# RWKV gate projection moved ahead of the recurrence, and the group norm written as factor times tile plus another tile

## Chip, cores and metric

One core of a Trainium2 chip runs the whole program. The metric is device microseconds of one execution, the median of several runs. Lower is better.

## What is computed

The reference is three transformer layers on 512 tokens of width 1024: an RWKV-7 layer with its MLP, a forgetting-attention layer with its MLP, and a hybrid sparse-attention layer with its MLP. The change touches the first layer's time mixing only. Cut to that:

```
g = sigmoid(x_g @ g1) @ g2                      # g1: 1024x160, g2: 160x1024
... y = recurrence over 512 tokens (16 heads of 64) ...
mean = mean(y over the head); var = mean(square(y - mean))
y = (y - mean) * rsqrt(var + GN_EPS)
y = y * lnx_w + lnx_b
bonus = sum(r * k * r_k over the head) * v
y = (y + bonus) * g
x = x + y @ w_o
```

## The kernel before

Activations lie transposed: a tile is 128 features by 512 tokens, and a full matrix is eight tiles (`DT`). Matrix products have float32 accuracy through three products of rounded parts: a weight block (128 x 1024) is split by GpSimd into `whi` and `wlo` (`split_hi`, `split_lo`), an activation into a high part (ScalarE, a rounding copy) and a low part (VectorE, a subtraction), and `three` issues high x high, high x low, low x high. A full output tile is 24 matmuls of 512 columns.

Weights come as one numbered stream of blocks in the order of `PHASES`: SyncE loads a block into one of four raw slots when GpSimd has split the block that was there, GpSimd splits it into one of two slots (`SPL`) when TensorE is done with the block before the last (`blk`), and TensorE waits for it on `split_ready`. Each engine's order is written out by hand, and semaphores tie the engines together.

The first layer runs in this order. A mixing stage prepares the inputs (`mix`, `mix_lo`) while TensorE makes k and r. Then come the eight value tiles (`for e in range(DT)` at line 693); between them `BETWEEN` puts the head sums of kk and of the bonus, and `kk_spread` hands the kk norm back to all rows. VectorE works meanwhile through a loop of eight (line 1872) that makes the operands of the recurrence and the bonus products (`bonus`; `bonus(i)` waits until the head sum of product i-2 is done, since two buffers `tmp` alternate). TensorE then transposes k, b and v to token order (`tokens`), and the recurrence follows in four steps of two chunks of 64 tokens (`for n in range(QT)`), each a long chain of small matmuls with ScalarE and VectorE between them.

After the recurrence comes the norm stage. TensorE makes head means with the block matrix `bones`, VectorE subtracts them (`gn_c`), ScalarE squares, TensorE sums by head (`head_sums`), ScalarE takes the root, VectorE the reciprocal and its two parts (`head_recip`). In a loop of eight TensorE then spreads the factor over the rows (`spread`, a matmul with 48 rows) and makes a tile of the gate projection (six matmuls: two weight blocks, the second with 32 live rows of 128). For each tile VectorE multiplies by the spread factor, ScalarE applies `lnx_w` and `lnx_b` (`gn_aff`), VectorE adds the bonus (`BON`) and multiplies by the gate out of PSUM (`y_gated`), ScalarE makes the high part and VectorE the low part. When all are through, `linear("rwkv_o", ...)` makes the eight output tiles one after another, and the residual, the next norm and the MLP follow. The gate's hidden values `sgF` get their parts `sgH` and `sgL` at the start of the norm stage. The two gate blocks are numbers 30 and 31 of the stream; GpSimd splits them in the last step of the recurrence, as its loop over the recurrence's masks stands ahead of them. The loads of x and of block 32 onward wait for the end of the recurrence (`rec_done`).

## Time and profile before

| | us |
|---|---|
| median of 3 runs | 2460.22 (2455.23 to 2460.65) |
| profiled execution, its own time | 2465.94 |
| its span in the trace | 2464.1 |
| TensorE busy (matmuls) | 2354.1, 96% of the span |
| VectorE busy | 1189.3, 48% |
| ScalarE busy | 573.7, 23% |
| GpSimd busy | 1289.0, 52% |

The profile is of one execution. A row of the page's groups gives line, engine, operation, tiles, count, busy time and the mean of one. The "chain that ended last" follows the last instruction back, at each step to what released it. A timeline row is start, length, engine, line and operation, and in brackets how long the engine had been idle and for whom. The granted clock is the share of TensorE's full speed (2.4 GHz); 0.50 is its lower level, 1.2 GHz. PE is TensorE, DVE VectorE, ACT ScalarE, POOL GpSimd.

### The profile page before, as it was taken

What the parts mean: (1) busy time and instruction counts of PE and PEld (TensorE: products, weight loads), DVE (VectorE), ACT (ScalarE), POOL (GpSimd) and SP (SyncE); (2) the same over time, 40 slices, a digit from 0 to 9 for tenths busy, and PEclk for the clock granted to TensorE, in tenths of its full rate; (3) what the DMA queues carried; (4) which work ended last, traced back from release to release, by engine and by line L of the source; (5) the groups of instructions that cost most, each with busy time, mean ns of one, the idle gap of its engine ahead of it and who ended that gap; (6) DMA issues with size and microseconds to landing.
All of it is one profiled execution on the core that took longest, in us unless ns stands there. A gap on an engine that the chain in (4) does not pass through costs nothing.

```text
span 2464.1 us, 41824 instructions
## 1 busy us (share of the span) xinstructions
PE 2354.1 (96%) x16908; PEld 1886.9 (77%) x16908; DVE 1189.3 (48%) x1483; ACT 573.7 (23%) x1168; POOL 1289.0 (52%) x839
## 2 busy tenths in 40 slices
PE   6988999899999999989999999999999999999999
PEld 4765888578888877766788888787877777888887
DVE  8858433475343352667543334518045656633333
ACT  4541333221010122144311111101015441201100
POOL 4652001056666655555566666566544545666665
PEclk9998999879999999999999999999998998999999
DMA  3220000122223222201222322223321111222222
GB/s 143 83 72 25 3 3 3 69 68 95 94 94 102 94 91 76 89 20 35 69 94 95 101 94 94 94 94 112 111 85 44 44 35 66 96 96 94 99 96 85
DMA packets 50448, 188.37 MB, mean 76 GB/s; under 512 B 5617, under 2 KB 5745, under 8 KB 49809
## 3 DMA queue, kind: packets, MB, share of 16 engines
q1 hardware_dynamic: 49824, 183.40, 22.2%
q10 hardware_dynamic: 496, 3.12, 0.4%
q8 instruction: 99, 1.62, 0.3%
q14 instruction: 29, 0.23, 0.0%
HBM read 184.33 MB, written 2.10 MB: 76 GB/s over the span
## 4 chain that ended last, share of the span: by engine, by line
PE 85%; DVE 10%; issue 2%; ACT 2%; POOL 0%; DMA 0%; ACTq 0%; DVEq 0%; SPq 0%; POOLq 0%
PE ps L593 23%; PE ps L595 22%; PE ps L594 22%; PE ps L1099 2%; PE ps L1084 2%; PE ps L768 2%; PE ps L605 2%; DVE HL L1948 1%; PE ps L1065 1%; DVE ssq L1745 1%; PE ps L778 1%; PE ps L1066 1%; PE ps L776 1%; PE ps L761 1%; PE ps L754 1%
## 5 line engine op out<-in xcount | busy, mean ns | idle before, releaser
L439 POOL TENSOR_TENSOR wlo<-raw,whi 128x1024 fp32r<-128x1024 f32 (+1 forms) x355 | 828.3, 2333 | 26.4
L432 POOL TENSOR_SCALAR whi<-raw 128x1024 fp32r<-128x1024 f32 x336 | 362.5, 1079 | 816.9 <-PE ps L595 792.3
L593 PE MATMUL ps<-HH,whi 128*128 128x512 f32 x1312 | 529.7, 404 | 8.4 <-DVE HL L1948 8.4
L595 PE MATMUL ps<-HH,wlo 128*128 128x512 f32 x1312 | 514.3, 392 | 0.0
L594 PE MATMUL ps<-HL,whi 128*128 128x512 f32 x1312 | 513.9, 392 | 0.0
L593 PEld LDWEIGHTS ps<-HH,whi 128*128 128x128 f32 x1312 | 248.1, 189 | 69.8 <-DVE HL L1948 14.1
L593 PE MATMUL ps<-hidH,whi 128*128 128x512 f32 x768 | 298.8, 389 | 0.0
L594 PE MATMUL ps<-hidL,whi 128*128 128x512 f32 x768 | 298.8, 389 | 0.0
L595 PE MATMUL ps<-hidH,wlo 128*128 128x512 f32 x768 | 298.8, 389 | 0.0
L595 PEld LDWEIGHTS ps<-HH,wlo 128*128 128x128 f32 x1312 | 248.2, 189 | 52.9
L594 PEld LDWEIGHTS ps<-HL,whi 128*128 128x128 f32 x1312 | 248.6, 189 | 52.3 <-issue 4.3
L1995 DVE TENSOR_TENSOR X<-X,ps 128x512 f32<-128x512 f32 x192 | 123.3, 683 | 306.7 <-PE ps L595 306.7
L1481 ACT ACTIVATE sqrT<-relT 128x512 f32<-128x512 f32 x96 | 60.8, 634 | 792.0 <-DVE relT L1984 792.0
L1987 DVE TENSOR_TENSOR hidL<-sqrT,hidH 128x512 fp32r<-128x512 f32 x96 | 183.9, 1935 | 88.8 <-ACT hidH L1485 88.8
L1984 DVE SCALAR_TENSOR_TENSOR relT<-ps,rstd 128x512 f32<-128x512 f32 x96 | 66.4, 692 | 234.1 <-PE ps L595 234.0
L594 PEld LDWEIGHTS ps<-hidL,whi 128*128 128x128 f32 x768 | 144.2, 188 | 30.0
L595 PEld LDWEIGHTS ps<-hidH,wlo 128*128 128x128 f32 x768 | 144.2, 188 | 29.9
L593 PEld LDWEIGHTS ps<-hidH,whi 128*128 128x128 f32 x768 | 144.2, 188 | 29.9
L465 POOL TENSOR_TENSOR mRB<-mRB,cst 128x512 f32<-128x512 f32 x8 | 10.1, 1279 | 176.2 <-ACT mRB L1435 176.2
L494 POOL TENSOR_SCALAR prs<-prs,cls,GT 128x32 f32<-128x32 f32 (+4 forms) x48 | 32.9, 686 | 78.0 <-DVE cls L2122 66.0
L593 PE MATMUL ps<-mixH,whi 128*128 128x512 f32 x128 | 52.8, 412 | 11.8 <-DVE mixL L1811 8.9
L1310 ACT ACTIVATE HH<-X,vec 128x512 fp32r<-128x512 f32 x40 | 28.8, 721 | 144.0 <-DVE X L1955 71.2
(438 smaller groups left out, 3598.6 us busy)
## 6 DMA issues: line engine op xcount, KB each, us to landing
raw<-stream SPq DMA_DIRECT2D x336, 512.0 KB, 3.3
X<-xT SPq DMA_DIRECT2D x2, 1024.0 KB, 6.6
X<-xT SPq DMA_DIRECT2D x1, 2048.0 KB, 7.7
CW<-cmpw ACTq DMA_DIRECT2D x1, 2048.0 KB, 10.2
out<-X SPq DMA_DIRECT2D x4, 512.0 KB, 2.6
cst<-consts SPq DMA_DIRECT2D x1, 511.5 KB, 9.3
c2f<-consts ACTq DMA_DIRECT2D x1, 466.0 KB, 3.2
c2s<-consts ACTq DMA_DIRECT2D x1, 466.0 KB, 5.4
```

What stands on the lines that cost most here:

```text
L432: pool.tensor_scalar(whi[:, s, :, :], raw[:, j, :].rearrange("p (k m) -> p k m", k=DT), 1.0, 0.0, ALU.mult, ALU.add)\
L439: return pool.tensor_tensor(wlo[:, s, a:z, :], raw[:, j, a * P:z * P].rearrange("p (k m) -> p k m", k=z - a), whi[:, s, a:z, :].bitcast(F3 ...
L593: pe.matmul(acc, whi[:, s, k, :], hi, start=start, stop=False)
L594: pe.matmul(acc, whi[:, s, k, :], lo, start=False, stop=False)
L595: return pe.matmul(acc, wlo[:, s, k, :], hi, start=False, stop=stop)
L605: pe.matmul(ps[0:112, bank, :], gather_heads(i), tmp[i % 2][:, :], start=i == 0, stop=i == n - 1).then_inc(S(f"{tag}_sum"), 1)
L768: mm = pe.matmul(square(hp, 1 - c, hp, p), mN[half(c), hp, p, :], mT[half(c), hp, p, :], start=True, stop=True)
L1084: mm = pe.transpose(ps[0:w, 4 + hp, j * P:(j + 1) * P], B["P"][:, 2 * (u % 2) + hp, j * P:j * P + w], ident)
L1481: act.activation(sqrT[:, j % 2, :], relT[:, j % 2, :], ACT.Square).then_inc(S("full"), 1)
L1984: dve.scalar_tensor_tensor(relT[:, j % 2, :], ps[:, j, :], 0.0, rstd[:, :], ALU.max, ALU.mult).then_inc(S("rel"), 1)
L1987: dve.tensor_tensor(hidL[buf][:, j - 1, :], sqrT[:, (j - 1) % 2, :], hidH[buf][:, j - 1, :].bitcast(F32), ALU.subtract).then_inc(S("hid"), 1)
L1995: ins = dve.tensor_tensor(X[:, e, :], X[:, e, :], ps[:, 4 + 2 * (j % 2) + o, :], ALU.add)
```

## The change

- The parts `sgH` and `sgL` of the gate's hidden values are made in the mixing stage, and in another place of SBUF.
- The 48 matmuls of the gate projection stand behind the eighth value tile, ahead of the transposes. They wait for both gate blocks to be split and alternate between two PSUM banks; ScalarE copies each tile to a new buffer `G`, which lies where the four raw weight slots are. GpSimd splits the two gate blocks ahead of its work for the recurrence.
- The bonus head sums go from behind value tiles 2 to 5 to behind tiles 3 to 6.
- In each step of the recurrence VectorE makes two tiles of (bonus + `lnx_b`) x gate in place of the bonus.
- In the norm stage, head means and head sums are interwoven (four PSUM banks for the means). VectorE makes the tiles `YA` = (y - mean) x `lnx_w` x gate, four of them ahead of the reciprocal. In the loop it multiplies one by the spread factor and adds the other tile. ScalarE's affine step is gone.
- The raw slots are loaded again as the `YA` tiles release `G`: blocks 32 and 33, then x, then 34 and 35, and from there on as before.
- Two output tiles are made side by side: in each of the eight steps of the loop TensorE does the same k for tile 0 and tile 1, with the spread for a later tile behind it. The other six tiles follow one by one.
- The semaphore for `gn_a` shares one with `sg_split`.

```diff
@@ -213,8 +213,10 @@
...
 
-    sgH = at("sgH", [P, 2, T], zone(7), F32R)
-    sgL = at("sgL", [P, 2, T], zone(7, 4096), F32R)
+    sgH = at("sgH", [P, 2, T], zone(8, 8192), F32R)
+    sgL = at("sgL", [P, 2, T], zone(8, 12288), F32R)
+    G = at("G", full, zone(10))
+    YA = at("YA", full, zone(7))
     YH = at("YH", full, zone(1), F32R)
@@ -408,8 +410,12 @@
...
             sp.wait_ge(S("rec_done"), 1)
-            sp.dma_start(X[:, :, :], xT).then_inc(S("x_again"), 16)
-            with sp.Fori(pre, NBLK // RAW) as i:
+            for j in range(RAW):
+                sp.wait_ge(*count("gn_a", 2 * j + 2))
+                sp.dma_start(raw[:, j, :], stream[pre * RAW + j]).then_inc(S(f"raw_in{j}"), 16)
+                if j == 1:
+                    sp.dma_start(X[:, :, :], xT).then_inc(S("x_again"), 16)
+            with sp.Fori(pre + 1, NBLK // RAW) as i:
                 rest(0, RAW, i)
@@ -458,13 +464,13 @@
...
                 split(b, b % RAW, b // RAW)
-            splits(2 * RAW, START["gate_up"])
+            splits(2 * RAW, START["rwkv_o"])
             for n in range(QT):
...
                         .then_inc(S("rb_ready"), 1)
-            splits(START["gate_up"], START["kv_v"] + 4)
+            splits(START["rwkv_o"], START["kv_v"] + 4)
 
@@ -688,7 +694,7 @@
...
 
-            BETWEEN = [("kk", 0, 4), ("kk", 4, 8), ("bo", 0, 2), ("bo", 2, 4), ("bo", 4, 6), ("bo", 6, 8)]
+            BETWEEN = [("kk", 0, 4), ("kk", 4, 8), None, ("bo", 0, 2), ("bo", 2, 4), ("bo", 4, 6), ("bo", 6, 8), None]
             pe.wait_ge(S("mix_lo"), NMIX)
@@ -699,7 +705,7 @@
...
                     pe.wait_ge(S("rkv_read"), 16)
-                if e < len(BETWEEN):
+                if BETWEEN[e] is not None:
                     tag, first, end = BETWEEN[e]
@@ -707,6 +713,19 @@
...
 
+            g0 = START["gate_up"]
+            pe.wait_ge(S("split_ready"), g0 + 2)
+            pe.wait_ge(S("sg_split"), 1)
+            for e in range(DT):
+                if e < 2:
+                    pe.wait_ge(S("rkv_read"), 16 + 5 + e)
+                else:
+                    pe.wait_ge(S("g_copied"), e - 1)
+                mm = three(ps[:, e % 2, :], (g0 % SPL, e), sgH[:, 0, :], sgL[:, 0, :], True, False)
+                if e == 7:
+                    mm.then_inc(S("blk"), 1)
+                mm = three(ps[:, e % 2, :], ((g0 + 1) % SPL, e), sgH[:, 1, :], sgL[:, 1, :], False, True)
+                mm.then_inc(S("gate_up") if e < 7 else S("blk"), 1)
             pe.wait_ge(S("kk_used"), DT)
@@ -781,6 +800,7 @@
...
 
+            pe.wait_ge(S("g_copied"), DT)
             for n in range(QT):
@@ -968,26 +988,37 @@
...
 
-            g0 = START["gate_up"]
-            for i in range(DT):
-                pe.wait_ge(S("y_done"), NCH)
-                if i >= 2:
-                    pe.wait_ge(S("gn_c"), i - 1)
-                pe.matmul(ps[:, i % 2, :], const("bones"), Rr[:, i, :], start=True, stop=True).then_inc(S("gn_mean"), 1)
-            head_sums("gn", DT)
-            ready(g0 + 1)
-            pe.wait_ge(S("sg_split"), 1)
-            for e in range(DT):
-                spread("gn", e, [2, 3], gnR)
-                if e >= 2:
-                    pe.wait_ge(S("y_gated"), e - 1)
-                mm = three(ps[:, 6 + e % 2, :], (g0 % SPL, e), sgH[:, 0, :], sgL[:, 0, :], True, False)
-                if e == 7:
+            pe.wait_ge(S("y_done"), NCH)
+            for i in range(DT + 3):
+                if i < DT:
+                    if i >= 4:
+                        pe.wait_ge(S("gn_c"), i - 3)
+                    pe.matmul(ps[:, i % 4, :], const("bones"), Rr[:, i, :], start=True, stop=True).then_inc(S("gn_mean"), 1)
+                if i >= 3:
+                    head_sum("gn", i - 3, DT)
+
+            def y_tile(e, bank, k):
+
+                mm = three(ps[:, bank, :], ((START["rwkv_o"] + e) % SPL, k), YH[:, k, :], YL[:, k, :], k == 0, k == DT - 1)
+                if k == DT - 1:
                     mm.then_inc(S("blk"), 1)
-                mm = three(ps[:, 6 + e % 2, :], ((g0 + 1) % SPL, e), sgH[:, 1, :], sgL[:, 1, :], False, True)
-                mm.then_inc(S("gate_up") if e < 7 else S("blk"), 1)
+
+            for i in range(3):
+                spread("gn", i, [2, 3], gnR)
+            ready(START["rwkv_o"] + 1)
+            for k in range(DT):
+                pe.wait_ge(S("y_lo"), k + 1)
+                for e in range(2):
+                    y_tile(e, e, k)
+                if k + 3 < DT:
+                    spread("gn", k + 3, [2, 3], gnR)
             pe.wait_ge(*count("gn_used", DT))
-            linear("rwkv_o", YH, YL, ("y_lo", 0), ("x_up", 0), [])
+            for e in range(2, DT):
+                ready(START["rwkv_o"] + e)
+                if e >= 4:
+                    pe.wait_ge(S("x_up"), e - 3)
+                for k in range(DT):
+                    y_tile(e, e % 4, k)
             mlp(0, 1, HH, HL)
@@ -1370,7 +1401,8 @@
...
                     act.wait_ge(*count("g_sum", 1))
-                    mark(act.activation(sgF[:, :, :], sgF[:, :, :], ACT.Sigmoid), "sg_ready")
+                    link(act.activation(sgF[:, :, :], sgF[:, :, :], ACT.Sigmoid), "sg_ready")
+                    mark(act.activation(sgH[:, :, :], sgF[:, :, :], ACT.Copy), "sg_hi")
                 if 4 <= n < 8:
@@ -1414,6 +1446,13 @@
...
             v_read(7)
+            act.wait_ge(S("split_ready"), START["rwkv_o"])
+            for e in range(DT):
+                if e < 7:
+                    act.wait_ge(S("gate_up"), e + 1)
+                else:
+                    act.wait_ge(S("blk"), START["gate_up"] + 2)
+                mark(act.activation(G[:, e, :], ps[:, e % 2, :], ACT.Copy), "g_copied")
             for u in list(range(16)) + list(range(16, 24, 2)):
@@ -1501,20 +1540,15 @@
...
             act.sem_inc(S("rec_done"), 1)
-            mark(act.activation(sgH[:, :, :], sgF[:, :, :], ACT.Copy), "sg_hi")
             for i in range(DT):
...
             head_root("gn", DT, 5, epsg)
-            for i in range(DT + 1):
-                if i < DT:
-                    act.wait_ge(*count("gn_used", i + 1))
-                    mark(act.activation(Rr[:, i, :], Rr[:, i, :], ACT.Identity, scale=vcol("lnx_w", i), bias=vcol("lnx_b", i)), "gn_aff")
-                if i:
-                    act.wait_ge(S("y_gated"), i)
-                    mark(act.activation(YH[:, i - 1, :], tmp[(i - 1) % 2][:, :], ACT.Copy), "y_hi")
+            for i in range(DT):
+                act.wait_ge(S("y_gated"), i + 1)
+                mark(act.activation(YH[:, i, :], tmp[i % 2][:, :], ACT.Copy), "y_hi")
             norm_squares(1, "m0", "mlp_g", 0, HH)
@@ -1835,6 +1869,9 @@
...
                     link(dve.tensor_copy(pselR[:, :, :], pselF[:, :, :]))
+                if n == 8:
+                    dve.wait_ge(S("sg_hi"), 1)
+                    mark(dve.tensor_tensor(sgL[:, :, :], sgF[:, :, :], sgH[:, :, :].bitcast(F32), ALU.subtract), "sg_split")
                 if 2 <= n < 6:
@@ -1931,6 +1968,10 @@
...
                     mark(dve.tensor_tensor(mRK[:, hp, :, :], pair_of(2 + 2 * hp, 0), wide(mRK, "leT"), ALU.mult), "gram_read")
+                if n == 0:
+                    dve.wait_ge(S("g_copied"), DT)
+                for i in (2 * n, 2 * n + 1):
+                    link(dve.scalar_tensor_tensor(BON[:, i, :], BON[:, i, :], vcol("lnx_b", i), G[:, i, :], ALU.add, ALU.mult))
                 for c in range(2):
@@ -2012,27 +2053,29 @@
...
 
-            dve.wait_ge(S("sg_hi"), 1)
-            mark(dve.tensor_tensor(sgL[:, :, :], sgF[:, :, :], sgH[:, :, :].bitcast(F32), ALU.subtract), "sg_split")
+            def gated(i):
+                mark(dve.scalar_tensor_tensor(YA[:, i, :], Rr[:, i, :], vcol("lnx_w", i), G[:, i, :], ALU.mult, ALU.mult), "gn_a")
+
             for i in range(DT):
                 dve.wait_ge(S("gn_mean"), i + 1)
-                mark(dve.scalar_tensor_tensor(Rr[:, i, :], ps[:, i % 2, :], -1.0 / HD, Rr[:, i, :], ALU.mult, ALU.add), "gn_c")
+                mark(dve.scalar_tensor_tensor(Rr[:, i, :], ps[:, i % 4, :], -1.0 / HD, Rr[:, i, :], ALU.mult, ALU.add), "gn_c")
+            dve.wait_ge(S("gn_c"), DT)
+            for i in range(4):
+                gated(i)
             head_recip("gn", gnR)
...
                 if n < DT:
+                    dve.wait_ge(*count("gn_a", n + 1))
                     dve.wait_ge(*count("gn_spread", n + 1))
-                    mark(dve.tensor_tensor(Rr[:, n, :], Rr[:, n, :], ps[:, 2 + n % 2, :], ALU.mult), "gn_used")
+                    mark(dve.tensor_tensor(YA[:, n, :], YA[:, n, :], ps[:, 2 + n % 2, :], ALU.mult), "gn_used")
+                if n + 4 < DT:
+                    gated(n + 4)
                 i = n - 1
                 if 0 <= i < DT:
-                    dve.wait_ge(S("gn_aff"), i + 1)
-                    link(dve.tensor_tensor(Rr[:, i, :], Rr[:, i, :], BON[:, i, :], ALU.add))
-                    if i < 7:
-                        dve.wait_ge(S("gate_up"), i + 1)
-                    else:
-                        dve.wait_ge(S("blk"), START["gate_up"] + 2)
+                    dve.wait_ge(*count("gn_used", i + 1))
                     if i >= 2:
-                        dve.wait_ge(S("y_hi"), i - 1)
-                    mark(dve.tensor_tensor(tmp[i % 2][:, :], Rr[:, i, :], ps[:, 6 + i % 2, :], ALU.mult), "y_gated")
+                        dve.wait_ge(S("y_lo"), i - 1)
+                    mark(dve.tensor_tensor(tmp[i % 2][:, :], YA[:, i, :], BON[:, i, :], ALU.add), "y_gated")
                 i = n - 2
```

## Rows read from the trace of the kernel before

**Rows 1.** Page: busy time by engine, the chain's engines, GpSimd's two costliest groups.

```profile
PE 2354.1 (96%) x16908; PEld 1886.9 (77%) x16908; DVE 1189.3 (48%) x1483; ACT 573.7 (23%) x1168; POOL 1289.0 (52%) x839
...
PE 85%; DVE 10%; issue 2%; ACT 2%; POOL 0%; DMA 0%; ACTq 0%; DVEq 0%; SPq 0%; POOLq 0%
...
L439 POOL TENSOR_TENSOR wlo<-raw,whi 128x1024 fp32r<-128x1024 f32 (+1 forms) x355 | 828.3, 2333 | 26.4
L432 POOL TENSOR_SCALAR whi<-raw 128x1024 fp32r<-128x1024 f32 x336 | 362.5, 1079 | 816.9 <-PE ps L595 792.3
```

**Rows 2.** Busy time by stretch (us, busy us and instructions by engine, clock, DMA), norm and projection.

```profile
481.00:495.00 14.00, 14.00 (x29) 8.15 (x28) 7.82 (x12) 5.14 (x7) 0.00 (x0) 0.50 0.00 0
495.00:510.00 15.00, 14.37 (x29) 8.40 (x28) 11.15 (x17) 5.77 (x8) 1.54 (x2) 0.50 0.00 0
520.00:540.00 20.00, 20.00 (x90) 16.53 (x89) 12.82 (x10) 4.98 (x8) 13.89 (x8) 1.00 0.24 79
```

**Rows 3.** Chain that ended last, 458 to 559 us: start, length, what.

```profile
458.19 1.06 ACT sgH L1504
...
461.25 1.96 PE ps L976 x4
...
467.15 7.41 PE ps L605 x16
474.58 0.70 ACT rstd L1469
...
484.31 0.72 PE ps L618
485.03 0.72 PE ps L593
485.76 0.43 PE ps L594
...
509.37 2.88 issue
...
558.60 0.57 issue
```

**Rows 4.** Timeline of TensorE, 205 to 262 us: start, length, instruction, idle before.

```profile
209.80 2.05 PE L605 MATMUL ps<-tmpB,cst 128*112 128x512 f32 x2 [5.08 <-DVE tmpB L1857]
...
217.98 0.39 PE L594 MATMUL ps<-mixVL,whi 128*128 128x512 f32 x1
...
220.25 0.39 PE L595 MATMUL ps<-mixVH,wlo 128*128 128x512 f32 x1
...
240.95 5.35 PE L681 MATMUL ps<-cst,Kk 128*128 128x128 f32 x32 [4.70 <-DVE boR L1861]
246.13 3.69 PE L681 MATMUL ps<-cst,AG 128*128 128x128 f32 x32
...
258.73 1.98 PE L754 MATMUL ps<-KR,AG 64*64 64x128 f32 x64 [0.84 <-issue]
```

**Rows 5.** Timeline of GpSimd ahead of the recurrence.

```profile
222.25 2.72 POOL L439 TENSOR_TENSOR wlo<-raw,whi 128x1024 fp32r<-128x1024 f32 x1
```

**Rows 6.** Timeline of VectorE: mixing, ahead of the recurrence, inside it.

```profile
112.61 0.69 DVE L1811 TENSOR_TENSOR mixVL<-mixM,mixVH 128x512 fp32r<-128x512 f32 x1 [2.01 <-ACT mixVH L1344]
...
221.18 4.34 DVE L1885 TENSOR_TENSOR KR<-KR,DEC 128x512 f32<-128x512 f32 x2
...
391.82 0.69 DVE L1938 COPY mN<-ps 64x512 f32<-64x512 f32 x1 [3.48 <-PE ps L845]
```

**Rows 7.** Busy time by stretch, transposes ahead of the recurrence.

```profile
242.00:244.00 2.00, 2.00 (x11) 2.00 (x10) 0.00 (x0) 1.49 (x3) 0.00 (x0) 0.50 0.00 0
246.00:248.00 2.00, 2.00 (x21) 2.00 (x20) 0.00 (x0) 2.00 (x6) 0.00 (x0) 1.00 0.00 0
```

**Rows 8.** Timeline of ScalarE, mixing.

```profile
76.01 0.63 ACT L1344 ACTIVATE mixH<-mixM 128x512 fp32r<-128x512 f32 x1 [3.58 <-PE ps L595]
```

**Rows 9.** Chain that ended last, last step of the recurrence.

```profile
409.09 1.71 issue
```

2 lines of the change are left out of this document (1 added, 1 removed).

## Prediction

> **What bounds the kernel now.** I read the page first, then the busy time by stretch, the chain that ended last, and last each engine's timeline in the two places that the change touches. TensorE is busy for 96% of the span and holds 85% of the chain, so an instruction added to its queue costs its own length unless it falls into one of its few waits [rows 1]. The group norm is where those waits are, and it is slow for another reason too: from 481 to 510 us TensorE has hardly a gap, yet its granted clock is 0.50 (the level of 1.2 GHz), while the projection that follows runs at 1.00 [rows 2]. In the chain the stage reads like this: the recurrence is over at 458.2; TensorE makes means and head sums until 474.58; square root, reciprocal and splitting hold it until about 480.7 (one step ahead of the second step's 484.31); then come eight steps, each a spread matmul (0.72) and six gate matmuls (the first 0.72, the others 0.43), 3.6 us a step; then 2.88 us for the next split weights; the output projection ends at 558.60 [rows 3]. The other place is ahead of the recurrence. TensorE finishes the last value tile at 236.25, waits 4.70 us for VectorE, starts its transposes at 240.95 at the low clock, and begins the recurrence at 258.73 [rows 4].
>
> **The gate projection ahead of the recurrence.** 48 matmuls of 512 columns move from the norm to behind the last value tile. One takes 0.227 us at the full clock (11 starts, 217.98 to 220.25, ten steps) [rows 4] and 0.43 at the low one [rows 3]. They cannot start when the value tiles end: they need both gate blocks split, the second split may begin only when the last value tile is done with its slot, and a split is 1.08 + 2.33 us in the mean [rows 1], its second part 2.72 beside a busy VectorE [rows 5]. With the hand-overs I take 3.8 us here and 3.6 in the norm.
>
> The start of that split also moves, because the bonus sums go to one value tile later. I followed the four queues through it. TensorE no longer sits 5.08 us in front of tile 5 for the bonus product [rows 4], and the first spreads come 1.7 us sooner; but VectorE's bonus products for tiles 4 and 6 now stand in front of head sums that come only after value tiles 4 and 5, which I count as waits of 3.3 and 1.7 us, with TensorE waiting some 4 us in turn for the second spread of each pair. Net, the last value tile ends about 1.5 us later, at 237.7. VectorE's chain ends at about 246 instead of 240.9, with two more collisions with a split; such a collision holds a VectorE operation with both inputs in SBUF until GpSimd's instruction ends (4.34 us for two products that take 0.69 each alone) [rows 6]. That lies beside the gate matmuls.
>
> So: second gate block split at 237.7 + 3.8 = 241.5. After such a wait the clock is low for about 4 us (0.50 at 242 to 244 after the wait of 4.70, and back at 1.00 from 246 on) [rows 7]: 48 matmuls take 48 x 0.227 + 2.0 = 12.9 us, and the transposes start at 254.5, 13.6 us later than now. ScalarE's copies (about 0.6 us each) keep up with 1.4 us per tile. The transposes win 1.7 back, since they start at the full clock (32 of them took 5.35 us at the low clock and 3.69 at the high) [rows 4]. **Recurrence later by 11.9 us.** Bounds: 10 (the two collisions do not happen) to 20 (the gate matmuls stay at the low clock, 48 x 0.43 = 20.6 us).
>
> The rows say the clock rose between 244 and 246 while nothing but transposes ran [rows 7]. The Trainium skill (TensorE: Matmul & The Clock Gate, Part 4) says that transposes do not count as activity for the clock; this trace disagrees. By that rule the clock could fall again in the 9 us of transposes and the 1.7 us would be lost, a bill of 13.6 instead of 11.9; the sum goes by the rows.
>
> **What goes beside it.** The rounding copy of the gate's hidden values (1.06 on ScalarE now, in the norm [rows 3]) goes to the mixing stage, where ScalarE waits 3.58 us right behind the sigmoid [rows 8]; its VectorE part, of a similar length, goes where VectorE waits 2.01 us soon after [rows 6]. Cost 0, at most 1 if a split collides. The eight products bonus-plus-bias times gate go into the recurrence, two a step, 1.3 to 1.5 us, into a wait of 3.48 us for TensorE [rows 6]: 0; without that cover 8 x 0.7 = 5.6. The two gate blocks' splits leave the last step of the recurrence. TensorE has an unexplained 1.71 us of issue there and a low clock behind it [rows 9]; I take no gain, and keep 3.5 us to either side, since the instruction stream shifts.
>
> **The norm.** Means and sums: today TensorE starts the bulk of the means at 461.25 because VectorE splits first. Afterwards 8 means of 0.98 and 8 sums of 0.93 run interwoven from 458.2 [rows 3]: 15.3 us, end 473.5, 1.1 sooner. VectorE makes four of the new factor tiles meanwhile. Square root, reciprocal, cast and low parts take 6.1 us as today, but the weights stream now restarts when factor tiles 2 and 4 are made (about 472 and 473.4), so that two splits run from 475.5 to 483 beside the low parts: I add 1.3, roots ready at 480.8, no gain.
>
> The loop: per tile VectorE has a factor product (first four), the spread product, the bonus sum and the low part; at 0.6 to 0.7 an operation 2.6 us a step, later 1.9. The first low part is there at about 487.9. Up to then TensorE has three spreads and nothing else, so it starts low. Then a step is six matmuls, and a spread for five of the eight: 0.72 + 0.72 + 5 x 0.43 = 3.6, which is today's step exactly [rows 3]. I take it that the clock does as in the same pattern today and stays at 0.50; TensorE, not VectorE, then sets the pace. 8 x 2.58 + 5 x 1.02 = 25.7, less 1.8 because the last three steps have no spread and are a plain stream of matmuls, like those that regain the clock today: end 511.9. (With no such recovery the stage is 1.8 longer.) This holds two output tiles of eight. The third needs a slot that tile 0 gives back at 511.2: split 3.6, start 514.8. Six tiles of 24 matmuls at 0.227 are 32.8, plus 0.8 for a clock that may have fallen: 548.4 against 558.6. **Norm and output projection shorter by 10.2, less what follows.** X is fetched again behind two blocks rather than first, and is wanted only after 510; 0. Off this come 0.5 us, since VectorE's first low part meets the second of the two splits: -9.7.
>
> Sum: +11.9 - 9.7 = **+2.2 us**. It is made against the profiled execution (span 2464.1, time 2465.94), which lies 5.7 above the median of 2460.22; on the median it gives **2462**.
>
> **The rivals.** *The clock rises in the loop* (0.20). The pattern is today's but the operands are others: the gate's second block is mostly padding, the output's is not. If that is what tells, TensorE reaches 1.00 some 4 us in; VectorE paces the loop, last low part at about 500.4, end 502.5, third tile at 505.3, end near 539: -19. With +11.9 this is -7, 2453, and with the issue gap of rows 9 gone -10.6. For it: the plain streams of value and key tiles regained the clock within some 4 us. Against it: 29 us of today's loop at 0.50 [rows 2]. The Trainium skill (same page, Part 1) says that sustained activity releases the throttle; by it this rival would be the forecast.
>
> *The gate matmuls stay low* (0.15). The same cause would hold them low ahead of the recurrence: 20.6 us instead of 12.9, +9.9, 2470. If the loop's clock then rises it is nearly paid back.
>
> *A slower front* (0.14). VectorE's and TensorE's waits in the value tiles feed on each other; one more wait round of about 4 us, with the clock lost behind it (2 us) in both of the last tiles, makes +8 to +12: 2468 to 2472. It decides from 5 us on.
>
> *The front is nearly hidden* (0.07). Only if value tiles end 3 us sooner than now, which takes away both collisions and waits: +6, total -4 with a plain loop and -11 with the issue gap gone.
>
> The forecast, a bill and a gain of one size, has 0.44.
>
> **How the numbers follow.** A measurement of this kernel tells about 0.3%, 7.4 us, from no change. The forecast (2456 to 2467) is no change. Of the first rival's 0.20 about 0.13 lies under 2452.8; of the second's 0.15, 0.11 over 2467.6; of the third's 0.14, 0.12; of the fourth's 0.07, 0.05 lies under. Faster 0.18, same 0.59, slower 0.23. Range 2449 to 2473: the loop at the full clock with the gap gone below, a low gate block or slow front with 3.5 us above.
>
> **What would show it.** First recurrence matmul at 270 to 271 (under 267 or over 275 is a failed step); the gate matmuls at 1.00 after some 4 us; the eight new products inside VectorE's waits; step length of the recurrence unchanged; roots ready 22 to 23 us after the recurrence; a step of 3.6 us and granted clock 0.50 in the loop (1.4 to 2.6 us and 1.00 is the first rival); a wait of about 3 us ahead of the third output tile; output projection done 90 us after the recurrence instead of 100. The forecast is wrong if one of the two large terms is off by more than 7 us while the other holds.

## The result, and the profile after

| | median us | range | ratio to before | 95% interval |
|---|---|---|---|---|
| before | 2460.14 | 2455.23 to 2460.65 | | |
| changed | 2478.49 | 2475.54 to 2481.76 | 1.0087 | 1.0068 to 1.0105 |

The change makes the kernel slower: 18 us between the medians, 17 to 26 us by the ratio's interval (the ratio is the recorded one; the two medians alone give 1.0075). I had forecast no change, 2462, with 2473 as the upper end, so the result is outside the range.

The two profiled executions show only 9.6 us of it (2475.54 against 2465.94): that of before lies 5.8 above the median of its kernel, that of the changed kernel 2.9 below. The traces therefore serve to place the cost, and the medians of the experiments to size it.

The page of the changed kernel, its busy time and the engines of the chain that ended last:

```profile
PE 2346.0 (95%) x16908; PEld 1884.3 (76%) x16908; DVE 1198.4 (48%) x1491; ACT 571.6 (23%) x1168; POOL 1290.5 (52%) x839
...
PE 86%; DVE 10%; issue 2%; ACT 2%; POOL 1%; DMA 0%; DVEq 0%; SPq 0%; POOLq 0%; ACTq 0%
```

TensorE is busy for 8 us less than in [rows 1] while the span is 9.6 us longer (2473.7). So the engine did not get more work, it got new waits, and the page as a whole does not say where. The timeline of TensorE ahead of the recurrence does, for the first part (start, length, instruction, idle before and for whom):

```profile
207.91 0.79 PE L695 MATMUL ps<-kkR,pselR 48*128 48x512 f32 x1 [4.33 <-DVE KR L1911]
...
222.86 0.49 PE L695 MATMUL ps<-kkR,pselR 48*128 48x512 f32 x1 [4.27 <-DVE KR L1911]
...
242.93 0.50 PE L599 MATMUL ps<-sgH,whi 128*128 128x512 f32 x1 [4.25 <-POOL wlo L445]
...
255.59 3.65 PE L687 MATMUL ps<-cst,Kk 128*128 128x128 f32 x32
...
271.95 1.98 PE L773 MATMUL ps<-KR,AG 64*64 64x128 f32 x64 [0.84 <-issue]
```

The last value tile is done at 242.93 - 4.25 = 238.68 (forecast 237.7), the split is awaited for 4.25 (3.8), the gate matmuls take 12.66 (12.9), the transposes start at 255.59 (254.5), and the recurrence starts at 271.95 (270.6). The two waits of some 4 us for the second spread of a pair are there. The front costs 271.95 - 258.73 = 13.2 us where 11.9 was forecast [rows 4].

VectorE in the same stretch:

```profile
232.48 2.77 DVE L1913 TENSOR_TENSOR AG<-AG,RD 128x512 f32<-128x512 f32 x1
...
239.08 1.02 DVE L1917 TENSOR_SCALAR KR<-KR 128x8 f32<-128x8 f32 x1
...
241.31 2.12 DVE L1912 TENSOR_TENSOR AG<-AG,KR 128x512 f32<-128x512 f32 x1
...
245.46 1.41 DVE L1898 TENSOR_TENSOR boR<-ps,boR 16x512 fp32r<-16x512 f32 x2
```

Its chain ends at 245.46 + 1.41 = 246.87 (forecast 246) instead of just ahead of 240.95 [rows 4]. The first three operations above, which run beside the two added splits, take 4.4 us more than the same ones elsewhere in this trace (0.69, 0.17 and 0.69). TensorE, which is in its gate matmuls until 255.59, does not wait for this chain.

The chain that ended last, from the end of the recurrence to the end of the output projection:

```profile
470.12 3.70 PE ps L996 x8
...
484.34 0.70 ACT rstd L1508
...
492.39 0.81 PE ps L624
...
498.82 0.61 DVE YL L2082
...
532.56 1.05 POOL whi L438
...
570.80 0.57 issue
```

Recurrence: 470.12 - 271.95 = 198.2 us, against 199.5 from [rows 3, 4]; its first three steps take 146.7 us against 146.0 before (146.0 in changed_again), so the new products cost at most 0.8. The issue gap of [rows 9] with the low clock behind it is not there; the last step has one of 1.26 us at another place, at 1.00. Roots: the first spread runs 22.3 us after the recurrence (means and sums 1.1 us shorter than forecast, cast and low parts longer), the first low part is done at 499.43, where the forecast has 487.9 + 11.9 = 499.8. Then it goes apart. The forecast gives tile 0's slot back at 511.2 + 11.9 = 523.1; the chain reaches GpSimd's next split at 532.56, 9.5 us later. From the end of the recurrence to the end of the projection are 100.7 us, against 100.4 before [rows 3]: the gain of 9.7 is not there at all. At 570.80 the kernel is 12.2 behind, which is +13.2 - 1.3 + 0.3. The span is only 9.6 longer, because 2.6 us come back much later: by stretches, the trace of before has the clock at 0.50 from 1850 to 1853, where that of the changed kernel, 13 us further on, has 1.00. I take that as one execution against another and not as the change; no run isolates it.

TensorE inside the loop:

```profile
499.56 0.77 PE L599 MATMUL ps<-YH,whi 128*128 128x512 f32 x1 [4.74 <-DVE YL L2082]
...
510.99 0.80 PE L599 MATMUL ps<-YH,whi 128*128 128x512 f32 x1 [2.05 <-DVE YL L2082]
...
513.85 0.79 PE L624 MATMUL ps<-gnR,pselR 48*128 48x512 f32 x1
516.69 0.79 PE L599 MATMUL ps<-YH,whi 128*128 128x512 f32 x1 [2.05 <-DVE YL L2082]
...
519.55 0.79 PE L624 MATMUL ps<-gnR,pselR 48*128 48x512 f32 x1
522.39 0.51 PE L599 MATMUL ps<-YH,whi 128*128 128x512 f32 x1 [2.05 <-DVE YL L2082]
```

The five steps from 499.56 to 526.97 take 6.34, 5.09, 5.70, 5.70 and 4.58 us, 5.5 in the mean and not 3.6, and each begins with a wait for VectorE's low part. The shorter ones have some matmuls at the full clock, since the granted clock rises twice in the loop and falls again (columns as in [rows 2]):

```profile
503.00:506.00 3.00, 0.28 (x2) 0.10 (x1) 2.55 (x4) 0.63 (x1) 0.00 (x0) 0.96 0.10 18
```

 The waits read alone look like a VectorE that is too slow. VectorE's own timeline says otherwise:

```profile
488.44 1.73 DVE L2012 CAST gnR<-rstd 112x512 fp32r<-112x512 f32 x1
490.20 2.13 DVE L1898 TENSOR_TENSOR gnR<-rstd,gnR 16x512 fp32r<-16x512 f32 x2
...
514.75 0.69 DVE L2070 TENSOR_TENSOR YA<-YA,ps 128x512 f32<-128x512 f32 x1 [3.81 <-PE ps L624]
515.35 0.68 DVE L2078 TENSOR_TENSOR tmpA<-YA,BON 128x512 f32<-128x512 f32 x1
515.96 0.68 DVE L2082 TENSOR_TENSOR YL<-tmpB,YH 128x512 fp32r<-128x512 f32 x1
520.45 0.69 DVE L2070 TENSOR_TENSOR YA<-YA,ps 128x512 f32<-128x512 f32 x1 [3.81 <-PE ps L624]
```

In the steps of 5.70 VectorE works 1.9 us and waits 3.81 for TensorE's spread; TensorE works 3.65 and waits 2.05 for VectorE. Both wait, each for the other, in turn.

**My theory from here: a ring of two queues.** The spread for tile k+3 stands in TensorE's queue behind the six matmuls of step k. The low part of tile k+1 stands in VectorE's queue behind the product with that spread, in the same round of its loop (round n = k+3: product for tile n, bonus sum for tile n-1, low part for tile n-2). And step k+1 waits for the low part of k+1. So nothing overlaps: 516.69 to 519.55 matmuls, 0.90 until the spread's product starts at 520.45, 1.94 for product, sum and low part, and the next step at 522.39: 2.86 + 0.90 + 1.94 = 5.70. The rivals: the low clock alone, VectorE's work alone, and a dearer front than the trace shows.

### The profile page after: what moved, and what is told of

Its sections match the earlier page's. It is cut to its first block, busy times and chain, and to the rows that moved or that the text cites. A ratio compares the mean times of both kernels' runs of the same rounds, so it can differ in the third digit from the quotient of the medians.

```text
span 2473.7 us, 41835 instructions
## 1 busy us (share of the span) xinstructions
PE 2346.0 (95%) x16908; PEld 1884.3 (76%) x16908; DVE 1198.4 (48%) x1491; ACT 571.6 (23%) x1168; POOL 1290.5 (52%) x839
## 4 chain that ended last, share of the span: by engine, by line
PE 86%; DVE 10%; issue 2%; ACT 2%; POOL 1%; DMA 0%; DVEq 0%; SPq 0%; POOLq 0%; ACTq 0%
PE ps L599 23%; PE ps L600 23%; PE ps L601 23%; PE ps L1115 2%; PE ps L1130 2%; PE ps L787 2%; PE ps L611 1%; DVE HL L1989 1%; DVE ssq L1779 1%; PE ps L1096 1%; PE ps L1097 1%; PE ps L797 1%; PE ps L795 1%; PE ps L780 1%; PE ps L773 1%
```

## Experiments

Every kernel was timed beside runs of before on its own chip; the fourth column is taken against the median of before in the same batch (2461.46, 2460.76 or 2460.13).

| kernel | median us | range | over the median of before | ratio to before | 95% interval |
|---|---|---|---|---|---|
| changed_again | 2479.22 | 2476.17 to 2481.73 | +17.8 | 1.0077 | 1.0059 to 1.0094 |
| spread_first | 2466.10 | 2462.65 to 2472.07 | +4.6 | 1.0025 | 1.0013 to 1.0037 |
| four_spread_banks | 2465.57 | 2458.92 to 2471.45 | +4.8 | 1.0026 | 1.0016 to 1.0036 |
| bonus_sums_early | 2475.83 | 2472.41 to 2477.70 | +14.4 | 1.0060 | 1.0043 to 1.0077 |
| gate_first_halves | 2477.90 | 2475.43 to 2480.66 | +16.4 | 1.0072 | 1.0055 to 1.0089 |
| gates_left_out | 2473.39 | 2470.84 to 2474.15 | +13.3 | 1.0053 | 1.0038 to 1.0069 |
| warm_loop | 2463.46 | 2459.32 to 2468.27 | +2.7 | 1.0011 | 1.0002 to 1.0020 |
| factors_between_means | 2463.95 | 2461.63 to 2469.18 | +3.8 | 1.0018 | 1.0009 to 1.0027 |
| front_mended | 2461.10 | 2456.38 to 2463.01 | +0.3 | 1.0003 | 0.9991 to 1.0014 |
| all_mended | 2451.60 | 2449.12 to 2458.97 | -8.5 | 0.9963 | 0.9949 to 0.9977 |
| before_warm_loop | 2452.83 | 2451.13 to 2457.23 | -7.9 | 0.9971 | 0.9959 to 0.9983 |
| before_warm_parts_inside | 2448.81 | 2447.92 to 2450.48 | -11.3 | 0.9956 | 0.9943 to 0.9970 |

**changed_again**: the changed kernel with no edit, as the base for the others.

> The changed kernel itself, unaltered, as the measure for the three beside it on the same chip. The profile showed +12 to +13 us in the touched stretch and the medians +18. If the rest is chance between executions, these rounds give +13 to +18 over the kernel before and the new profile again shows about +13 at the end of the output projection; if the rest is a steady cost somewhere else, this profile shows it as a difference that opens after the output projection.

It repeats the result (the medians differ by 0.7 us). At the end of the output projection its trace is 14.8 us behind that of before and at the very end 11.9, so no further cost opens behind the projection; that the medians show 18 is left to the scatter between executions. Its trace has the recurrence at 274.10 instead of 271.95, with one more stretch at the low clock ahead of it (0.50 from 154 to 157 us, where the first trace has 1.00). So much does the front differ between two executions.

**spread_first**: the same matmuls in another order.

```diff
             for k in range(DT):
                 pe.wait_ge(S("y_lo"), k + 1)
-                for e in range(2):
-                    y_tile(e, e, k)
                 if k + 3 < DT:
                     spread("gn", k + 3, [2, 3], gnR)
+                for e in range(2):
+                    y_tile(e, e, k)
```

> The spread for tile k+3 is issued ahead of the six matmuls of step k instead of behind them; nothing else. Theory (a closed ring: low part k+1 stands behind the product with spread k+3 in VectorE's queue, and spread k+3 stands behind the matmuls of step k in TensorE's, so the two engines take turns at 5.7 us a step): the step falls to what TensorE alone needs at the low clock, about 3.6 us or less, the loop from 33 us to about 24, 8 to 10 us less than the changed kernel. Rival (the low clock of the loop is what costs, the order is not): the step stays over 5 us and the time moves by less than 3 us.

13.1 us faster than changed_again (8 to 10 forecast) by two statements that change places. Its chain, one step of the loop, and its busy time by stretch (us, busy us and instructions of PE, PEld, DVE, ACT, POOL, granted clock, DMA share, GB/s):

```profile
506.10 0.72 PE ps L624
506.82 0.72 PE ps L599
...
509.68 0.72 PE ps L624
```

```profile
503.00:510.00 7.00, 7.00 (x15) 4.21 (x14) 4.44 (x7) 1.26 (x2) 0.00 (x0) 0.50 0.58 193
510.00:520.00 10.00, 10.00 (x21) 6.24 (x21) 6.01 (x10) 1.89 (x3) 0.00 (x0) 0.50 0.06 24
```

The step is 3.58 us, TensorE has no gap, and the clock is 0.50: what the forecast had assumed of the change itself. The trace shows 9.9 us of the 13.1 by the time of the first residual; the rest is not placed. From the end of the recurrence to the end of the projection it is 92.0 us, against 100.4 before and 102.2 in changed_again; the forecast has 90.7.

The order of VectorE's queue is unchanged, so a ring is left, but without the six matmuls: the spread now waits for low part k, and low part k+1 waits for the product with that spread. At the low clock it is shorter than TensorE's own 3.58 and does not show.

**four_spread_banks**: the order stays, but spreads go to four PSUM banks and run four ahead, which opens the ring at another place.

```diff
-            for i in range(3):
-                spread("gn", i, [2, 3], gnR)
+            for i in range(4):
+                spread("gn", i, [2, 3, 6, 7], gnR)
...
-                if k + 3 < DT:
-                    spread("gn", k + 3, [2, 3], gnR)
+                if k + 4 < DT:
+                    spread("gn", k + 4, [2, 3, 6, 7], gnR)
...
-                    mark(dve.tensor_tensor(YA[:, n, :], YA[:, n, :], ps[:, 2 + n % 2, :], ALU.mult), "gn_used")
+                    mark(dve.tensor_tensor(YA[:, n, :], YA[:, n, :], ps[:, (2, 3, 6, 7)[n % 4], :], ALU.mult), "gn_used")
```

> The changed kernel with its order kept (the spread stays behind the matmuls of a step) but four PSUM banks for the spreads and four of them issued ahead of the loop. Theory (a closed ring of two engines): the ring is now two steps long, so a step costs half of 5.7 and TensorE's 3.6 at the low clock binds again: the same time as with the spread first, 2464 to 2469. Rival (the gain of spread first came from the place of the spread beside the weight loads, not from the ring): a step stays at 5.7 us, 2476 to 2481.

```profile
510.00:520.00 10.00, 10.00 (x22) 6.37 (x22) 6.52 (x11) 2.29 (x4) 0.00 (x0) 0.50 0.02 8
```

2465.57, inside the forecast 2464 to 2469, the same time over before as spread_first (+4.8 against +4.6) and the same gapless 0.50. The two edits are not independent: both put the spread for tile k+3 between steps k-1 and k, one step sooner than the changed kernel. They differ in the banks (four against two), in how many spreads stand ahead of the loop, and in the side of the wait for the low part on which the spread stands. What they share is that the six matmuls are out of the ring. VectorE's work is the same in both and in the changed kernel, so it was not VectorE's amount of work; and the two faster kernels lie at 0.50 throughout, while the slow one rises above it twice, so it was not the clock.

**bonus_sums_early**: head sums of the bonus in the places where before has them.

```diff
-            BETWEEN = [("kk", 0, 4), ("kk", 4, 8), None, ("bo", 0, 2), ("bo", 2, 4), ("bo", 4, 6), ("bo", 6, 8), None]
+            BETWEEN = [("kk", 0, 4), ("kk", 4, 8), ("bo", 0, 2), ("bo", 2, 4), ("bo", 4, 6), ("bo", 6, 8), None, None]
```

> The changed kernel with the bonus head sums back behind value tiles 2 to 5. My reading of the front: the later sums cost about 1.5 to 2 us in the end of the last value tile; so the gate matmuls start 1 to 3 us sooner and the time falls by as much. Rival (the sums' place is neutral, or better late): the start of the gate matmuls moves by less than 1 us, or to later.

```profile
209.30 1.96 PE L611 MATMUL ps<-tmpB,cst 128*112 128x512 f32 x2 [5.14 <-DVE tmpB L1894]
...
240.10 0.79 PE L599 MATMUL ps<-sgH,whi 128*128 128x512 f32 x1 [4.42 <-POOL wlo L445]
```

3.4 us between the medians (1 to 3 forecast); the intervals of the two kernels overlap, and the start of the gate matmuls is the firmer sign. The wait of 5.08 of [rows 4] is back (5.14), but the two waits of 4.3 are gone but for 0.91. The gate matmuls start at 240.10 instead of 242.93 (245.11 in changed_again). I had priced the new order at 1.5.

**gate_first_halves**: the matmuls of the first gate block, for four tiles in four banks, stand inside the wait for the second block's split.

```diff
-            pe.wait_ge(S("split_ready"), g0 + 2)
+            pe.wait_ge(S("split_ready"), g0 + 1)
...
+                if e == 3:
+                    pe.wait_ge(S("split_ready"), g0 + 2)
...
-                mark(act.activation(G[:, e, :], ps[:, e % 2, :], ACT.Copy), "g_copied")
+                mark(act.activation(G[:, e, :], ps[:, e % 4, :], ACT.Copy), "g_copied")
```

> The changed kernel with the first-block matmuls of four gate tiles issued while the second gate block is still being split (four PSUM banks instead of two). Theory (the wait for the second block's split, about 4 us, and the low clock behind it stand uncovered in the front): 12 of 48 matmuls go into the wait, 2.7 us, and up to 2 us of low clock go too: the recurrence starts 2.5 to 4.5 us sooner. Rival (the front waits for VectorE's chain anyway): no change, under 1 us.

```profile
245.04 0.50 PE L599 MATMUL ps<-sgH,whi 128*128 128x512 f32 x1 [1.56 <-POOL wlo L445]
...
249.09 0.49 PE L599 MATMUL ps<-sgH,whi 128*128 128x512 f32 x1 [0.69 <-ACT G L1464]
```

A miss: 1.3 us, within the scatter. The wait shrinks from 4.24 (changed_again) to 1.56 and the clock stays at 1.00 behind it, but the win is given back in four waits of 0.69 to 0.75 for ScalarE's copies, since the order that I wrote lets a first half wait for a bank that was only just filled.

**gates_left_out**: 39 of the 48 gate matmuls are left out, so that the gate's values are not those of the reference; nine stay, and so do the waits and copies.

```diff
-                mm = three(ps[:, e % 2, :], (g0 % SPL, e), sgH[:, 0, :], sgL[:, 0, :], True, False)
                 if e == 7:
-                    mm.then_inc(S("blk"), 1)
-                mm = three(ps[:, e % 2, :], ((g0 + 1) % SPL, e), sgH[:, 1, :], sgL[:, 1, :], False, True)
-                mm.then_inc(S("gate_up") if e < 7 else S("blk"), 1)
+                    pe.matmul(ps[:, e % 2, :], whi[:, g0 % SPL, e, :], sgH[:, 0, :], start=True, stop=False).then_inc(S("blk"), 1)
+                pe.matmul(ps[:, e % 2, :], whi[:, (g0 + 1) % SPL, e, :], sgH[:, 1, :], start=e < 7, stop=True)\
+                    .then_inc(S("gate_up") if e < 7 else S("blk"), 1)
```

> The changed kernel with 39 of the 48 gate matmuls ahead of the recurrence left out (the gate's values are wrong, one matmul per tile stays, and the wait for both splits stays). It prices the front: my reading is 11 to 13 us of matmuls, of which 39/48 go, and that VectorE's chain, done some 6 us after the gates start, is only just hidden. Theory: the transposes start at VectorE's end, 6 to 8 us sooner than in the changed kernel, and no more; so of a front of 13 to 15 us about 5 to 7 remain, which are the later end of VectorE's chain. Rival (the front is matmuls alone): 39 x 0.227 = 9 us or more.

TensorE, and VectorE:

```profile
249.06 4.71 PE L687 MATMUL ps<-cst,Kk 128*128 128x128 f32 x32
```

```profile
245.87 1.41 DVE L1897 TENSOR_TENSOR boR<-ps,boR 16x512 fp32r<-16x512 f32 x2
```

4.5 us less over before than changed_again, 5.1 less than the first measurement. Neither the theory nor the rival comes out. The nine matmuls that stay take 5.7 us (243.34 to 249.06), since the clock is 0.50 from 245 on and there are three waits for ScalarE's copies (0.51, 0.20, 0.20). The transposes start behind them at 249.06 and not at the end of VectorE's chain, which is over 1.8 us sooner (247.28); TensorE never waits for it.

The recurrence starts at 266.32, 5.6 us sooner than in the changed kernel and 7.6 later than in [rows 4]. The 7.6 are: the last value tile 2.8 later, the wait for the split 0.4 shorter than the wait that it replaces, 5.7 for the nine matmuls, transposes and bonus spreads 0.5 faster. VectorE's longer chain is hidden here too. It is a floor only: without the last nine matmuls as well, the transposes could start at most 1.8 us sooner. How much of it is due to the splits and how much to the bonus order this run doesn't tell.

**warm_loop**: spread_first, and matmuls on constants, written to a PSUM bank that nobody reads, while TensorE waits.

```diff
+            def filler(n):
+                for _ in range(n):
+                    pe.matmul(ps[:, 4, :], pselR[:, 0, :], pselR[:, :, :], start=True, stop=True)
...
+            filler(40)
             for i in range(3):
                 spread("gn", i, [2, 3], gnR)
+            filler(15)
             ready(START["rwkv_o"] + 1)
```

> Spread first, and in addition 40 matmuls on constants, whose result nobody reads, in TensorE's wait for the roots, and 15 more behind the first three spreads. They add work and compute nothing. Theory (the 10 us wait for the roots takes the clock down, and the pattern of the loop doesn't bring it back): the granted clock stays 1.00 through the loop, VectorE sets the step at 2.0 to 2.6 us, the loop ends 6 to 9 us sooner than with the spread first alone. Rival (the loop itself holds the clock down): the clock falls inside the loop again, 0 to 2 us.

```profile
503.00:508.00 5.00, 3.87 (x15) 2.30 (x13) 3.29 (x6) 1.26 (x2) 0.00 (x0) 1.00 0.20 54
508.00:513.00 5.00, 4.08 (x15) 2.46 (x14) 3.78 (x6) 1.26 (x2) 0.00 (x0) 1.00 0.78 292
513.00:518.00 5.00, 4.08 (x15) 2.46 (x15) 3.92 (x7) 1.26 (x2) 0.00 (x0) 1.00 0.00 2
```

From 503 on the loop runs at 1.00 and its step is 2.55 (spreads at 507.62, 510.17, 512.72, 515.27). Neither engine fills it:

```profile
510.17 0.50 PE L624 MATMUL ps<-gnR,pselR 48*128 48x512 f32 x1 [0.46 <-DVE YL L2089]
```

```profile
510.78 0.69 DVE L2077 TENSOR_TENSOR YA<-YA,ps 128x512 f32<-128x512 f32 x1 [0.66 <-PE ps L624]
```

This is the ring that spread_first has left: 0.61 from the spread to its product, then 1.94 for product, sum and low part, together 2.55.

The constants did not hold the clock all the time. It fell to 0.50 from 499 to 502, at the start of the second row, and was back at 1.00 from 503, before the loop's matmuls began:

```profile
499.00:503.00 4.00, 4.00 (x11) 2.96 (x11) 4.00 (x7) 0.63 (x1) 0.00 (x0) 0.57 0.33 90
```

The theory of the clock holds, its gain of 6 to 9 us does not: over before it is 1.9 us better than spread_first. In the traces the stage from the end of the recurrence to the end of the projection is 5.0 us shorter (87.0 against 92.0), which is five steps shorter by 1.03, but its recurrence ends 1.6 us later, ahead of anything that the edit changes. The third tile still waits 3.17 for its split.

**before_warm_loop**: the same remedy in the kernel before.

```diff
             head_sums("gn", DT)
+            filler(26)
             ready(g0 + 1)
```

> The kernel before, with 26 matmuls on constants in TensorE's wait for the roots (6.1 us), whose result nobody reads; they compute nothing. If the clock lost in that wait is what keeps the loop of before at 3.6 us a step, the clock stays at 1.00, VectorE's four operations per tile set the step at about 2.8 to 3.1, and the kernel is 4 to 7 us faster than before. Rival (the loop holds the clock down by itself): 0.50 again in the loop and no change.

```profile
481.00:488.00 7.00, 6.70 (x25) 4.19 (x24) 4.92 (x9) 2.29 (x4) 0.00 (x0) 1.00 0.00 0
488.00:495.00 7.00, 6.10 (x23) 3.61 (x22) 6.89 (x12) 4.31 (x6) 0.00 (x0) 1.00 0.01 2
```

```profile
487.25 0.69 DVE L2030 TENSOR_TENSOR KR<-KR,ps 128x512 f32<-128x512 f32 x1
...
489.18 0.68 DVE L2045 TENSOR_TENSOR YL<-tmpA,YH 128x512 fp32r<-128x512 f32 x1
489.78 0.68 DVE L2030 TENSOR_TENSOR KR<-KR,ps 128x512 f32<-128x512 f32 x1
```

7.9 us faster than before (4 to 7 forecast), for one line of code and its helper. Where [rows 2] show 0.50 the clock is 1.00, the step is 2.53 instead of 3.6 from the third tile on, and it is VectorE, without a gap, that now sets it. The rewrite was forecast to win 9.7 us in the same stage for a bill of 11.9 in front; this wins 7.9 for no bill.

**factors_between_means**: spread_first with the factor tiles made between the mean subtractions rather than behind them, so that the raw slots are released, loaded and split earlier.

```diff
+                if i >= 4:
+                    dve.wait_ge(S("gn_c"), i - 3)
+                    gated(i - 4)
             dve.wait_ge(S("gn_c"), DT)
-            for i in range(4):
-                gated(i)
```

> Spread first, and the first four factor tiles are made between the mean subtractions instead of behind them, so that the weight loads restart some 4 to 6 us sooner and both splits are over before the roots are cast and split. Theory (the two splits hold VectorE in the cast and the low parts, 6.0 us in place of 1.8): roots ready about 4 us sooner, 2462 in place of 2466. Rival (the collisions move to the mean subtractions and cost the same there): under 1 us.

Its VectorE timeline at the roots, and that of spread_first:

```profile
490.14 1.11 DVE L2012 CAST gnR<-rstd 112x512 fp32r<-112x512 f32 x1
491.28 1.40 DVE L1898 TENSOR_TENSOR gnR<-rstd,gnR 16x512 fp32r<-16x512 f32 x2
493.64 0.69 DVE L2071 TENSOR_TENSOR YA<-YA,ps 128x512 f32<-128x512 f32 x1 [0.95 <-PE ps L624]
```

```profile
489.76 1.80 DVE L2012 CAST gnR<-rstd 112x512 fp32r<-112x512 f32 x1
491.60 4.15 DVE L1898 TENSOR_TENSOR gnR<-rstd,gnR 16x512 fp32r<-16x512 f32 x2
496.70 0.69 DVE L2070 TENSOR_TENSOR YA<-YA,ps 128x512 f32<-128x512 f32 x1 [0.95 <-PE ps L624]
```

The low parts are back at 1.40 and the first product runs 3.1 us sooner. The medians differ by 2.2, but over before by only 0.8, with intervals that overlap: of the theory's 4 us the medians do not show half, and the price of the splits beside the roots is between nothing and some 2 us of the kernel's time.

**front_mended**: spread_first, the early bonus sums and a better order of gate halves (four first halves, then three second ones, then in turns).

```diff
+            pe.wait_ge(S("split_ready"), g0 + 1)
+            pe.wait_ge(S("sg_split"), 1)
+            for e in range(4):
+                gate_half(e, 0)
+            pe.wait_ge(S("split_ready"), g0 + 2)
+            for e in range(3):
+                gate_half(e, 1)
+            for e in range(4, DT):
+                gate_half(e, 0)
+                gate_half(e - 1, 1)
+            gate_half(7, 1)
```

> Spread first, the bonus sums early again, and the first-block halves of four gate tiles ahead of the wait for the second block, with the fifth tile's first half only behind the third tile's second, so that the copies out of PSUM keep ahead. From the runs so far: 2466 less 3.4 for the sums less 2 to 3.5 for the halves (the earlier form lost 0.7 us a tile to those copies): 2459 to 2462, level with the kernel before. Rival (these terms hide each other): over 2463.

1.0003: level with before, 2461.10 inside the forecast, and 4.3 less over before than spread_first.

**all_mended**: front_mended, the factors between the means, and 34 + 15 constant matmuls.

> The changed kernel with everything found: spread first, bonus sums early, first halves in the split's wait, factor tiles between the means, and 34 + 15 matmuls on constants in the waits of the norm, whose result nobody reads. From 2461.1 of the first three: less 3 to 4 for the collisions, less 3 for the clock: 2454 to 2456, better than the kernel before by 5, and level with or a little over the kernel before with the warm loop (2452.8), since the front's price stays. Rival (the terms overlap): 2458 or more.

2451.60, somewhat better than the forecast of 2454 to 2456, and 8.5 us faster than before; so at the place to which one line brings the old kernel (before_warm_loop, 7.9).

**before_warm_parts_inside**: before with 30 constant matmuls, and with the parts of the gate's hidden values made behind the mean subtractions instead of ahead of them, so that the means start at once.

```diff
             act.sem_inc(S("rec_done"), 1)
-            mark(act.activation(sgH[:, :, :], sgF[:, :, :], ACT.Copy), "sg_hi")
...
+                if i == 1:
+                    mark(act.activation(sgH[:, :, :], sgF[:, :, :], ACT.Copy), "sg_hi")
...
-            dve.wait_ge(S("sg_hi"), 1)
-            mark(dve.tensor_tensor(sgL[:, :, :], sgF[:, :, :], sgH[:, :, :].bitcast(F32), ALU.subtract), "sg_split")
             for i in range(DT):
                 dve.wait_ge(S("gn_mean"), i + 1)
                 mark(dve.scalar_tensor_tensor(Rr[:, i, :], ps[:, i % 2, :], -1.0 / HD, Rr[:, i, :], ALU.mult, ALU.add), "gn_c")
+            dve.wait_ge(S("sg_hi"), 1)
+            mark(dve.tensor_tensor(sgL[:, :, :], sgF[:, :, :], sgH[:, :, :].bitcast(F32), ALU.subtract), "sg_split")
```

> The kernel before with 30 matmuls on constants in the wait for the roots, and the gate's hidden values split behind the mean subtractions instead of ahead of them. The start of the means is then free at once: 1 us less than with the matmuls on constants alone (2452.8). Rival: the same time, as the sums pace the stage.

2448.81, the best of all kernels here, 11.3 under the 2460.13 of before in its batch, and 3.4 more than before_warm_loop wins, where 1 was forecast. The edit does not account for that. In the traces the stage behind the recurrence is only 0.5 us shorter than in before_warm_loop (89.8 against 90.3), but the recurrence is 3.9 us shorter (196.6 against 200.5): the issue gap of [rows 9] is still 1.71 us in before_warm_loop and 0.30 here, with the clock at 1.00 behind it. Nothing was changed at that place, and the prediction kept 3.5 us for this gap to either side. Four more constant matmuls were added as well; no run separates the three.

## Why the prediction was wrong

**The step that failed** is this sentence on the loop: "I take it that the clock does as in the same pattern today and stays at 0.50; TensorE, not VectorE, then sets the pace." Its first half holds and its second does not. I counted each engine's work for a step (3.6 and 1.9 to 2.6) and took the larger, which is right only if the two overlap. In the kernel before they do, because its spread stands ahead of the step's six matmuls; here the step runs through both queues one after the other, 2.86 + 0.90 + 1.94 = 5.70 at the low clock and 5.5 in the mean of five. I had the order of both queues before me and wrote for neither what stands ahead of the instruction that the other engine waits for. The price is 13.2 us by spread_first and 13.0 by four_spread_banks (from the column over before; by the intervals each is good to some 5 us), against a forecast of 0. That the ring is the cause is shown: with the same work in both queues, taking the six matmuls out of it brings the step to 3.58, and the trace of the changed kernel has both engines waiting in turn for just the 5.70.

**The norm otherwise.** With the matmuls out of the ring the step is 3.58 at 0.50, as priced. The roots were 22.3 us behind the recurrence (22 to 23 forecast), but 24.4 in spread_first; the third tile waits 3.18 (3.6). I gave the splits beside the roots 1.3 us. On VectorE they cost 2.0 in the trace of the changed kernel and 4.1 in that of spread_first (low parts 2.13 and 4.15 instead of 1.40, the cast 1.3 to 1.4 more in both). Means and sums, 14.2 us where I had 15.3, paid for part of it.

**The front.** Forecast +11.9, in the trace +13.2: the last value tile 2.4 later rather than 1.5, the wait for the split 0.45 shorter than the wait it replaces rather than 0.9, gate matmuls 12.66 rather than 12.9, transposes and bonus spreads 1.4 faster rather than 1.7. Changed_again has +15.4, so the front varies by 2 us with the execution. The clock stayed at 1.00 through the transposes (255 to 263 us), as the sum had it. The term that was mis-sized is the order of the bonus sums: 3.4 by its own experiment, not 1.5.

**Together.** With spread_first the kernel stands at 1.0025, 3 to 9 us behind before, where the sum says +2.2. Its trace is 4.8 us behind at the end of the projection: +15.5 in front, -2.3 in the recurrence, -8.4 in the norm and projection. The balance of a bill in front and a gain behind was about right, the forecast fails by the one term that was not in it. With the front mended too it is at 1.0003. The single edits add up: ring 13.2, bonus order 3.4, gate halves 1.3 make 17.9, and all three in one kernel (with a better order of the gate halves) give 17.8 - 0.3 = 17.5. With some 5 us of uncertainty in each, the close agreement is partly luck.

**The rivals.** *The clock rises in the loop*: not as priced. In the changed kernel it rose twice, for some 3 us each, and fell again; all of 503 to 520 in spread_first lies at 0.50 with TensorE busy for 17.00 of 17 us. The Trainium skill (TensorE: Matmul & The Clock Gate, Part 1) says that sustained activity releases the throttle; these 17 us without a gap did not show it, whereas the plain matmuls behind the last spread did: in the chain of spread_first they fall from 0.43 to 0.23 us at 522.9. *The gate matmuls stay low*: no. Their starts are 0.227 us apart from about 247 on, and the 48 took 12.66. *A slower front*: its mechanism is there, the waits of TensorE for VectorE at 4.33 and 4.27, but these were in my sum already, and the surplus was 1.3 to 3.5 us rather than the 6 to 10 over the forecast that it priced. The range ended at 2473 because no rival ended higher; none of them was a ring. *The front is nearly hidden*: no, +13.2 in the trace where it had +6.

**Free, as priced:** the parts sgH and sgL in the mixing stage: the low part took 3.31 us there beside a split, but nobody waited for it. The eight products in the recurrence cost at most 0.8 us in its first three steps.

## What to carry to other kernels

For a loop over two engines with queues of fixed order, do not take the larger of the two sums. Write down for every wait what stands ahead of the signalling instruction in its own queue, and follow this back; if the walk returns to the same step, the step costs at least the sum around the ring. An instruction that feeds the other engine goes ahead of the bulk of the step, or the ring gets more buffers. Then walk it again: the ring that is left sets the step once the rest gets faster, as the 2.55 of warm_loop.

Where TensorE waits and a loop at the low clock follows, first try a row of matmuls on constants in that wait: here it was worth 8 us in the kernel before, one line against a rewrite. And work that is moved takes its weights' splits along: here TensorE had to wait 4.25 us for the second one in the new place, and both held VectorE for 4.4.

## What the runs showed of the hardware

The granted clock does not follow how busy TensorE is at the moment. In spread_first it is 0.50 for 17 us with 17.00 us busy; in warm_loop it is 1.00 for 15 us with 12.03 busy and a gap in every step; in the loop of the changed kernel it is 0.96 from 503 to 506 with 0.28 busy. What came before differs: in spread_first almost 17 us (485.6 to 502.5) with only three spreads in them; in warm_loop mostly constant matmuls, of which the last 15 (499.28 to 504.42, without a gap) began at 0.50 and ended at 1.00. But the changed kernel came to its loop out of the same kind of wait as spread_first, and its clock did rise for a while. Why the gapless matmuls of spread_first did not bring the clock back is not shown.

A copy from SBUF to SBUF on VectorE (112 x 512, the rounding of the reciprocal) takes 0.43 us alone (before, at 478.69) and 1.73 to 1.80 beside a split on GpSimd (changed kernel and spread_first). I had expected this only of operations with two inputs in SBUF.
